# A guarded block for overflowing tokens: moved from behind the expert loop to ahead of the loop's last expert

## The reference, cut to what matters

```
h  = rmsnorm(x)
for each token: pick 1 of 4 groups, then the top 2 of its 8 experts, with weights w
for expert e, rows xb of its tokens:
    hb = silu(xb @ w_gate[e]) * (xb @ w_up[e])
    y[tokens] += (hb @ w_down[e]) * w
x = x + y
```

## Time and profile before

| | us |
|---|---|
| median of 3 runs | 1352.63 |
| lowest, highest | 1352.59, 1354.44 |
| the profiled execution | 1351.29 |
| its span, first to last instruction | 1349.4 |
| mean granted TensorE clock | 0.916 |
| PE busy | 1035.4 (77%) |
| DMA on the chain that ended last | 45% of the span |

### The profile page before, as it was taken

How to read it: one execution, slowest core, us unless ns; L and a number is a source line. 1 busy time by engine, 2 the same in 40 slices (tenths; PEclk the granted TensorE clock), 3 DMA queues, 4 the chain that set the end, 5 groups by cost and what they waited for, 6 DMA issues and landing times.

```text
span 1349.4 us, 31076 instructions
## 1 busy us (share of the span) xinstructions
PE 1035.4 (77%) x13804; PEld 813.3 (60%) x13804; DVE 451.7 (33%) x1012; ACT 294.9 (22%) x569; POOL 15.2 (1%) x25
## 2 busy tenths in 40 slices
PE   6999999988767666666676999978666667656677
PEld 6999999966545444444454756656454444435456
DVE  6554555652212111211212766532121111212127
ACT  5433344421100000000002655311000000000017
POOL 1000000000000000000000010000000000000000
PEclk9999999999988888888878999999878878878889
DMA  9995653499999999999999950799999999999991
GB/s 281 303 262 141 172 154 124 193 380 426 424 426 427 426 427 426 425 426 427 425 428 380 398 196 4 298 420 428 426 425 427 426 425 426 426 424 426 426 376 48
DMA packets 115819, 469.98 MB, mean 348 GB/s; under 512 B 4816, under 2 KB 79696, under 8 KB 90992
## 3 DMA queue, kind: packets, MB, share of 16 engines
q1 hardware_dynamic: 115008, 465.78, 86.5%
q0 software_dynamic: 688, 2.28, 0.5%
HBM read 467.00 MB, written 1.05 MB: 347 GB/s over the span
## 4 chain that ended last, share of the span: by engine, by line
DMA 45%; PE 44%; DVE 5%; ACT 3%; issue 3%; DVEq 0%; SPq 0%; ACTq 0%
DMA ring<-moe_w_down 39%; PE ps L1817 7%; PE ps L1840 6%; PE ps L1566 5%; PE ps L1567 5%; PE ps L1565 5%; DMA ring<-moe_w_up 3%; DMA ring<-moe_w_gate 3%; PE ps L1679 2%; PE ps L1704 2%; PE ps L1870 2%; ACT g_hi L849 1%; PE ps L1629 1%; PE ps L1605 1%; PE ps L1853 1%
## 5 line engine op out<-in xcount | busy, mean ns | idle before, releaser
L1817 PE MATMUL ps<-ring,scr 128*32 128x128 f32 x8192 | 288.0, 300 | 153.7 <-DMA ring<-moe_w_up 95.3
L1817 PEld LDWEIGHTS ps<-ring,scr 128*32 128x32 f32 x8192 | 250.8, 121 | 191.8 <-DMA ring<-moe_w_up 106.6
L1840 PE MATMUL ps<-ring,scr 128*32 128x256 f32 x1920 | 151.8, 466 | 110.6 <-DMA ring<-moe_w_down 97.0
L1840 PEld LDWEIGHTS ps<-ring,scr 128*32 128x32 f32 x1920 | 75.3, 129 | 170.0 <-issue 101.2
L1288 DVE TENSOR_TENSOR scr<-scr,ps 128x128 f32<-128x128 f32 x64 | 23.8, 371 | 432.7 <-PE ps L1817 432.7
L817 ACT COPY scr<-ps 32x256 f32<-32x256 f32 x128 | 46.8, 365 | 526.9 <-PE ps L1840 526.1
L1301 DVE COPY scr<-ps 32x256 f32<-32x256 f32 x128 | 53.3, 417 | 228.9 <-PE ps L1840 228.0
L1565 PE MATMUL ps<-hT_hi,w_qk_hi 128*128 128x256 f32 x368 | 104.4, 284 | 0.0
L1567 PE MATMUL ps<-hT_hi,w_qk_lo 128*128 128x256 f32 x368 | 103.7, 282 | 0.0
L1566 PE MATMUL ps<-hT_lo,w_qk_hi 128*128 128x256 f32 x368 | 103.6, 281 | 0.0
L810 ACT ACTIVATE scr<-ps 128x128 f32<-128x128 f32 x64 | 17.8, 278 | 275.7 <-PE ps L1817 275.7
(11 more groups left out here) (269 smaller groups left out, 1190.0 us busy)
## 6 DMA issues: line engine op xcount, KB each, us to landing
ring<-moe_w_gate SPq DMA_DIRECT2D x64, 2048.0 KB, 36.1
ring<-moe_w_up SPq DMA_DIRECT2D x64, 2048.0 KB, 35.9
ring<-moe_w_down SPq DMA_DIRECT2D x60, 2048.0 KB, 36.1
ring<-dsa_w_in SPq DMA_DIRECT2D x72, 512.0 KB, 6.9
ring<-ple_w_gate SPq DMA_DIRECT2D x4, 2048.0 KB, 37.3
ring<-dsa_w_out SPq DMA_DIRECT2D x2, 2048.0 KB, 14.1
scr<-moe_w_down SPq DMA_DIRECT2D x4, 1024.0 KB, 7.2
scr<-moe_w_down SPq DMA_DIRECT2D x8, 512.0 KB, 9.7
```

What stands on the lines that cost most here:

```text
L1817: mm = pe.matmul(bank(b)[CW * q:CW * q + CW, 0:P], xT[:, k, :], tile(t, KD, FF)[:, k, P * q:P * q + P], start=(k == 0), stop=(k == KD - 1))
L1840: mm = pe.matmul(bank(6)[CW * q:CW * q + CW, 0:T], e_hT[:, CW * j:CW * j + CW], down[j][:, T * q:T * q + T], start=(j == 0), stop=(j == FF ...
```

## The change

- The block, with its check, goes into the expert loop of PE, ACT and DVE, ahead of expert 7 of each pass (`if i == BODY - 1`). On ACT and DVE the check is made in all four passes. On PE it is made in the three passes of the hardware loop (`and not first`), and not in the straight first pass.
- `flag` gets one integer for each pass and layer. POOL zeroes all of them at the start; DVE writes the largest count of layer `l` into the last one, number `4 l + 3`, after a wait for POOL's memset. The engines read number `4 l + it`, with `it` the pass. So passes 0 to 2 always read zero and branch past the block, and pass 3 reads the count.
- The block's own buffers move: its weights land in two halves (`e_wide`, `e_wide_d`), one in `x_sb` and one in the scratch, so SP's part issues six DMAs for an expert and not three, and the semaphore thresholds double; `o_sil` and `o_hT` have other places. SP's check stays where it was and reads the last integer of the layer.

```diff
-        flag = sb("flag", [1, 2], I32)
+        flag = sb("flag", [1, 2 * ITERS], I32)
...
-        e_wide = scratch(0, KD, 512)
-        e_wide_d = scratch(0, FF // P, D)
+        e_wide = [part(x_sb.rearrange("p c n -> p (c n)"), 0, KD // 2, 512), scratch(256, KD // 2, 512)]
+        e_wide_d = [x_sb[:, :, :], scratch(256, FF // P // 2, D)]
...
-        o_sil = scratch(4352, TC, 512)
-        o_hT = scratch(5376, 4, P)
+        o_sil = scratch(5376, TC, 512)
+        o_hT = scratch(2304, 4, P)
...
+            pool.memset(flag[:, :], 0).then_inc(S("fills"), 1)
...
@@ spilled, DVE
-                dve.tensor_copy(flag[0:1, l:l + 1], cmax[0:1, :]).then_inc(S("flag_ready"), 1)
+                dve.wait_ge(S("fills"), 3)
+                dve.tensor_copy(flag[0:1, ITERS * (l + 1) - 1:ITERS * (l + 1)], cmax[0:1, :]).then_inc(S("flag_ready"), 1)
...
@@ load_overflow, SP
-                count = sp.value_load(flag[0:1, l:l + 1], min_val=0, max_val=T)
+                count = sp.value_load(flag[0:1, ITERS * (l + 1) - 1:ITERS * (l + 1)], min_val=0, max_val=T)
                 with sp.If(count > CAP):
-                    sp.wait_ge(S("scattered"), (NGRP + 1) * (l + 1))
+                    sp.wait_ge(S("pw_ready"), ITERS * (l + 1))
+                    sp.wait_ge(S(f"o_x{l}"), 2)
...
@@ experts, PE: the same is taken away behind the loop; ACT and DVE likewise
+                def overflow(it):
+
+                    pe.wait_ge(S("flag_ready"), l + 1)
+                    count = pe.value_load(flag[0:1, bass.ds(ITERS * l + it, 1)], min_val=0, max_val=T)
+                    with pe.If(count > CAP):
+                        pe.wait_ge(S(f"o_x{l}"), 2)
+                        with pe.Fori(0, NE) as e:
+                            for j, b in ((0, 4), (1, 6)):
+                                pe.wait_ge(S(f"o_landed{l}"), 32 * (3 * e + j + 1))
+                                for c in range(TC):
+                                    for k in range(KD):
+                                        mm = pe.matmul(bank(b + c), hT[:, k, c * P:(c + 1) * P], e_wide[k // 4][:, k % 4, :],
+                                                       start=(k == 0), stop=(k == KD - 1))
...
+                            for c in range(TC):
+                                pe.wait_ge(S(f"o_h{l}"), TC * e + c + 1)
+                                for j in range(FF // P):
+                                    mm = pe.transpose(bank(4)[:, j * P:(j + 1) * P],
...
+                                for n in range(2):
+                                    for j in range(FF // P):
+                                        mm = pe.matmul(bank(2 * c + n), o_hT[:, j, :], e_wide_d[j // 2][:, j % 2, 512 * n:512 * n + 512],
...
                 def expert(it, i):
 
                     first = isinstance(it, int)
+                    if i == BODY - 1 and not first:
+                        overflow(it)
```

More of the change, by code:

```diff
@@ L803, in experts @@
                 act.activation(dif, dif, ACT.Exp).then_inc(S("dexp_ready"), 1)
+                def overflow(it):
+                    act.wait_ge(S("flag_ready"), l + 1)
+                    count = act.value_load(flag[0:1, bass.ds(ITERS * l + it, 1)], min_val=0, max_val=T)
+                    with act.If(count > CAP):
+                        with act.Fori(0, NE) as e:
+                            for c in range(TC):
+                                act.wait_ge(S(f"o_gate{l}"), TC * e + c + 1)
+                                act.activation(o_sil[:, c, :], bank(4 + c), ACT.Silu,
+                                               scale=rstd[:, c:c + 1]).then_inc(S(f"o_silu{l}"), 1)
+                        act.wait_ge(S(f"o_down{l}"), NE + 1)
                 table(ACT.Silu)
@@ L807, in experts @@
                     for i in range(BODY):
+                        if i == BODY - 1:
+                            overflow(it)
                         e = NE * l + BODY * it + i
@@ L823, in experts @@
                             act.copy(p_w[:, :, bass.ds(T * it, T)], bank(7, TC, T)).then_inc(S("pw_copied"), 1)
[L824 to L832, removed]
             def final(c):
@@ L1280, in experts, with overflow @@
                 spilled(l)
+                def overflow(it):
+                    dve.wait_ge(S("flag_ready"), l + 1)
+                    count = dve.value_load(flag[0:1, bass.ds(ITERS * l + it, 1)], min_val=0, max_val=T)
+                    with dve.If(count > CAP):
+                        overflow_rows(l)
+                        with dve.Fori(0, NE) as e:
+                            for c in range(TC):
+                                dve.wait_ge(S(f"o_silu{l}"), TC * e + c + 1)
+                                dve.wait_ge(S(f"o_up{l}"), TC * e + c + 1)
+                                dve.scalar_tensor_tensor(out=o_sil[:, c, :], in0=o_sil[:, c, :],
+                                                         scalar=r_wo[:, c, bass.ds(e, 1)], in1=bank(6 + c),
+                                                         op0=ALU.mult, op1=ALU.mult).then_inc(S(f"o_h{l}"), 1)
+                                dve.wait_ge(S(f"o_turned{l}"), TC * e + c + 1)
+                                dve.tensor_copy(o_hT, bank(4, 4, P)).then_inc(S(f"o_hT{l}"), 1)
+                        dve.wait_ge(S(f"o_down{l}"), NE + 1)
                 with dve.Fori(0, ITERS) as it:
@@ L1319, in experts @@
                 link.leave(ITERS)
[L1320 to L1333, removed]
             def add_ple(l):
@@ L1879, in experts @@
                         expert(it, i)
[L1881 to L1894, removed]
-                            pe.wait_ge(S(f"o_h{l}"), TC * e + c + 1)
-                            for j in range(FF // P):
-                                mm = pe.transpose(bank(4)[:, j * P:(j + 1) * P],
-                                                  o_sil[:, c, :].rearrange("p (m j) -> p j m", j=FF // P)[:, j, :], ident)
-                            mm.then_inc(S(f"o_turned{l}"), 1)
-                            pe.wait_ge(S(f"o_hT{l}"), TC * e + c + 1)
-                            for n in range(2):
-                                for j in range(FF // P):
-                                    mm = pe.matmul(bank(2 * c + n), o_hT[:, j, :], e_wide_d[:, j, 512 * n:512 * n + 512],
-                                                   start=False, stop=True, skip_group_check=True)
-                        mm.then_inc(S(f"o_down{l}"), 1)
             def ple(l):
```

22 lines of the change are left out of this document (19 added, 3 removed).

## The result

| | before | after |
|---|---|---|
| median of 17 runs each, us | 1353.01 | 1354.91 |
| lowest, highest | 1350.28, 1355.32 | 1353.46, 1357.5 |
| the profiled execution | 1351.29 | 1353.87 |
| q8 packets (code) | 110 | 114 |

The ratio is 1.0018, 95% interval [1.0011, 1.0025]: 1.5 to 3.4 us more. The ratio is inside the 0.2% that the prediction called no change (its interval reaches a little past it), and the median lies within its range, but it isn't the +0.2 us that the sum gave. Something of about 2 us was missing from it. All ratios here leave out executions in the slow state, of which there was one of the kernel before (2153.1) and one of e3_far (1395.56).

A forecast was written before the change was run, and what follows sets the result against it. The prediction took the expert loop as bound by the weight stream, the rest by engines. Terms 0 + 0 + 0 + 0.2 on 1351.29 gave 1351.5 for the profiled execution; with 1.34 for the median, 1352.8, range 1350.8 to 1358.5.

The forecast's parts named there:

- Seam, 0: Between scatter and turn behind the expert loop, taking the check out gains 0 us on PE, ACT and DVE.
- Checks, 0: In the passes of the expert loop, the added checks on PE, ACT and DVE fit into idle time; cost 0.
- The page after the branch, 0: In up of expert 31, the next code piece comes after 5.7 us, before down's weights matter; cost 0.
- rival 1: In up of expert 31, the code piece behind the branch takes 7.7 to 9.6 us; middle +4, 1356.7; chance 0.22.
- Rival 2: At the branch before expert 31, PE waits for two code pieces; +9 to +10 us, 1362; chance 0.08.
- rival 3: At the seam, ACT and DVE release the scatter earlier; -2.8 us in all, 1350.0; chance 0.07.
- Code traffic, +0.2: In the weight stream, fetching the block's under 14 KB of code 6 times at 425 GB/s costs 0.2 us.

The follow-up runs named there:

- e3_far: The changed kernel with PE's block written twice, so that the branch passes 436 instructions; median 1360.76 us, ratio 1.0045.
- e1_noblock: The kernel before with check and overflow block cut out on PE, ACT and DVE; median 1352.72 us, ratio 0.9992.
- e4_check_only: The changed kernel with PE's block cut to its first wait, leaving the check and a short branch; median 1353.32 us, ratio 0.9996.
- e9_warm_before: The kernel before with two spare matmuls between gate and up of each pass's last expert; median 1354.40 us, ratio 1.0020.
- e12: The kernel before with 2048 one-byte memsets written out straight for GpSimd beside layer 0's experts; median 1357.04 us, ratio 1.0015.
- e2_pe_only: The changed kernel with the checks and blocks of ACT and DVE put back behind the loop; median 1355.40 us, ratio 1.0011.
- e7_long: The changed kernel with the gate and up part of PE's block written twice, 347 instructions; median 1359.35 us, ratio 1.0046.
- e5_pos5: The changed kernel with check and block ahead of expert 5 of each pass, not 7, on all three engines; median 1355.58 us, ratio 1.0017.
- e10: e1_noblock with two spare matmuls between gate and up of each pass's last expert; median 1354.13 us, ratio 1.0006.
- e6_short: The changed kernel with the down part left out of PE's block, 136 instructions in place of 219; median 1355.30 us, ratio 1.0016.
- e8_warm: The changed kernel with two spare matmuls between gate and up of each pass's last expert; median 1353.47 us, ratio 1.0004.
- e11_code: The kernel before with 4096 one-byte memsets written out straight for GpSimd beside layer 0's experts; median 1368.02 us, ratio 1.0123.

## Why the prediction was right, and which term was mis-sized

Point by point, by its own steps.

- *Seam, 0*: right; the rows after repeat those of before, and e1_noblock gains nothing that can be told.
- *Checks, 0*: right in the sum. Wait, load and branch do take longer than nothing: in layer 0 the gate at 483.63 follows the gather after 0.34 us of "issue". In e4_check_only it costs nothing that can be told.
- *The page after the branch, 0*: right in place and in mechanism, short in size, and lucky in the profiled execution. The edge is in up. The text's place of the check in its piece (130 and 115 instructions) doesn't follow from its own counts: 2404 and some 40 instructions, less the 242 and 12 before the first edge, are 154 and 128 into a piece, 219 further leaves 139 and 165, and the edge is then 6 and 18 matmuls into up; 6 and 19 were measured. The piece comes 6.7 to 7.5 us after the copies, not 5.7, and so over the 6.6 from which rival 1 was to decide. It stopped nothing in the last pass because the copies of expert 30 were over 11.75 and 12.68 us ahead of down's weights, where they were 10.1 ahead before. In the seven profiles without a long block in PE's loop (before, e1, e4, e9 to e12) they are 10.1 to 10.9 ahead at 13 of the 14 layer ends, and in those with such a block 10.1 to 13.4. With a lead of about 10 layer 0 of the changed kernel was 1.50 and 0.66 us late in its two earlier passes, and e2_pe_only, which has the same code on PE, 1.05 in one. So part of rival 1 can be in the price, up to about 1 us in an execution. How often it strikes in expert 31 isn't shown. e3_far and e7_long show the same mechanism where it is covered even less, +6 us each. Rival 2, and rival 3, did not happen.
- *Code traffic, +0.2*: this is the term that the runs show mis-sized. I priced six passings of the block by their bytes over all 16 engines' rate; the queue has four packets more (114 for 110), since the block at the seam is gone. But a piece isn't spread: it is one packet of 16,384 bytes, which takes 1.07 us, where a 16 KB packet of weights takes 0.61, and a tile is there only with its last mark. It measured about +1.0 us, as follows.

The price, from the marks. Over 75 tiles in a row near the end of each layer, the time that the eight late engines (their mean) and the eight early ones took (the place of the window differs by a tile or two between runs):

| | layer 0: late, early, pieces | layer 1: late, early, pieces |
|---|---|---|
| before | 373.91, 367.10, 37 | 374.26, 367.06, 39 |
| e1_noblock | 374.03, 367.15, 37 | 373.92, 367.12, 37 |
| e4_check_only | 374.13, 367.08, 38 | 374.42, 367.15, 38 |
| after | 374.51, 367.17, 40 | 374.70, 367.12, 41 |
| e5_pos5 | 374.81, 367.16, 41 | 374.81, 367.14, 42 |
| e3_far | 374.89, 367.09, 42 | 375.17, 367.26, 44 |

The early eight don't change. The late eight lose (373.91 - 367.10) x 8 / 37 = 1.47 us for each piece, and 1.4 to 1.6 in every row of the table, wherever the window is put. So a piece costs the mean of the late engines 1.47 / 8 = 0.18 us. Down the table, the late time rises by 0.16 to 0.19 us (slope of each layer's six rows) for each piece that one run has more than another. The change adds two to three pieces to each window, and (374.51 - 373.91) + (374.70 - 374.26) = +1.0 us; with both windows moved together by up to three tiles it is 0.6 to 1.2. That answers for about half of the measured 2.

The other half is not settled. Three things could hold it, and no run tells them apart.

- *Where a step falls.* The tile's time is the last engine's and not the mean: it goes on in steps. A tile follows the next at 4.89 us, and one in some fifteen at 5.5 to 6.3 (with a smaller step near it in most cases), when the turn comes to the engine that is already last. Over just these 75 tiles the last mark of before and after took the same, 374.7 us, so how much of the 1.0 reaches the end depends on where a step falls. From the 12th tile of layer 0, and from the 13th of layer 1, to the last mark of the layer's last tile, the two layers together took 833.9 to 834.4 us in the five profiles of before, e1, e4, e9 and e10, and 834.5, 836.6, 836.6, 833.7 and 834.5 in after, e2, e5, e6 and e8: a mean of 1.0 more, with a spread larger than that.
- *The clock in the tail.* The last down of a layer takes 1.93 or 3.3 to 3.64 us, and which differs from profile to profile. It was the longer one at 1 of the 6 layer ends of before, e1 and e4, and at 4 of the 8 of after, e2, e5 and e6, too few to tell. In three of those four a step had just made PE wait longer: 3.92 us (e2_pe_only) and 3.85 (e5_pos5) before down, and 3.87 before up in layer 1 of the changed kernel. e8_warm hinted at the clock and e9_warm_before spoke against its being all.
- *The late piece in up*, as said above, up to about 1 us in layer 0. e6_short, whose downs are all released by their weights, and e5_pos5 cost as much without it, but their intervals leave room for 1 us.

Shown is: the price is PE's in the main, it needs the block's length and not the check, it is there too two experts earlier in the pass, and the count of pieces, and with it the time of the eight late engines, grows with the block.

No version that computes all that is asked for beat the kernel before.

## What to carry to other kernels

In a kernel whose weights come over all DMA engines at full rate, price code by pieces on the most burdened engine and not by its bytes: here 46 pieces in layer 0 put the late eight engines 9 us behind the early ones, in a stage of 440, before any change was made. A block branched past in a loop is fetched all the same: the page has 108 pieces with PE's block cut away, 112 with 136 instructions, 114 with 219, 117 with 347 and 120 with 436. Keep it outside the loop; at 136 instructions it still cost about 2 us. And don't read the cover of a late piece from one profile: 1.6 us of lead more or less decided here. Nor take one experiment that moves the time as expected (e8_warm) for the cause before it has been made on the kernel without the change.

## What the runs showed of the hardware that I had not expected

- TensorE's code came over eight of the sixteen DMA engines in turn: eight marks fall behind, one after another, and the lengths of its packets repeat with a period of eight (1.07, 1.07, 1.06, 1.10, 1.10, 1.09, 1.02, 1.02 us). GpSimd's 8 KB pieces went over a single other one: 32 of them put it 22.5 us behind the fastest, 16 put it 11.8 behind. The extra lag costs nothing until it passes that of the eight (10 us here); then it costs all of itself: 1.7 us past the next mark with 16 pieces, where the kernel took 2 to 3 us more, and 12.6 with 32, where the profiled execution took 11.8 more and the median 15.
- GB/s over all engines doesn't show a lagging engine: the others run ahead into the ring. It shows at the end of the stage alone, where the last slice of the layer fell from 380 to 284 GB/s in e11_code.
- Code ahead is thin: a branch over 219 instructions lands within what is loaded, one over 347 or 436 waits 4.9 to 6.1 us in expert 31, before gate or a few matmuls into it.
